# A hybrid attention/SSD trunk on one core: first modulation by feature tile, three first units side by side, and a last residual with its gates on ScalarE

## What is computed

```
mod = silu(cond) @ w_mod[l] + b_mod[l]      # 9 pieces of 1024; cond differs for context and latent
h   = rmsnorm(x, norm_pre) * (1 + scale) + shift
x   = x + 0.5 * gate * rmsnorm(swiglu(h), norm_post)
```

## Time and profile before

| | |
|---|---|
| time, median of 3 runs | 2957.63 us (2953.05 to 2960.02) |
| the profiled execution's own time | 2956.48 us |
| its span in the profile | 2954.7 us |
| mean granted TensorE clock | 0.99 of 2.4 GHz |
| TensorE matmul busy | 97% of the span |
| TensorE's share of the chain that ended last | 85% |
| VectorE / ScalarE / GpSimd busy | 59% / 37% / 9% |

### The profile page before, as it was taken

One profiled execution on the slowest core, in us unless ns is written; L12 is line 12 of the kernel. 1 busy time (PEld: TensorE's weight loads), 2 busy tenths in 40 slices (PEclk: granted clock), 3 DMA queues, 4 the chain that ended last, 5 costly groups with the idle time before them and its releaser, 6 DMA issues.

```text
span 2954.7 us, 47164 instructions
## 1 busy us (share of the span) xinstructions
PE 2854.5 (97%) x19366; PEld 2703.4 (91%) x19366; DVE 1753.5 (59%) x2640; ACT 1107.5 (37%) x1750; POOL 254.4 (9%) x201
## 2 busy tenths in 40 slices
PE   8999999998799999999999999999979999999997
PEld 5999999986589999999999999999945699999997
DVE  6567666647666555657564646457778747432334
ACT  5311126446865211146211126753334446211123
POOL 0000002000020000011000002000048511000002
PEclk9999999999999999999999999999999999999998
DMA  6545444420034544443543434632221133322233
GB/s 227 164 147 188 143 147 140 153 71 31 23 122 136 162 138 138 148 149 116 160 157 121 152 110 135 176 98 76 68 75 33 58 106 118 113 85 67 75 104 114
DMA packets 106968, 350.33 MB, mean 119 GB/s; under 512 B 11137, under 2 KB 29825, under 8 KB 106497
## 3 DMA queue, kind: packets, MB, share of 16 engines
q1 hardware_dynamic: 101122, 338.27, 36.1%
q10 hardware_dynamic: 5632, 9.05, 0.9%
HBM read 336.66 MB, written 10.62 MB: 118 GB/s over the span
## 4 chain that ended last, share of the span: by engine, by line
PE 85%; DVE 6%; ACT 3%; issue 3%; POOL 3%; DMA 0%; ACTq 0%; SPq 0%; DVEq 0%; POOLq 0%
PE P L1680 79%; PE P L1631 2%; ACT pb L884 1%; POOL mraw L687 1%; PE P L1739 1%; POOL toff L691 1%; DVE wl L1123 1%; DVE st L1253 0%; DVE xl L1163 0%; DVE xs L1425 0%; PE P L1883 0%; DVE st L1257 0%; DVE toff L1460 0%; PE P L2005 0%; DVE ft L1155 0%
## 5 line engine op out<-in xcount | busy, mean ns | idle before, releaser
L1680 PE MATMUL P<-xh,wh 128*128 128x320 f32 x4016 | 1018.4, 313 | 7.8 <-DVE xl L1163 6.6
L1680 PE MATMUL P<-xh,wl 128*128 128x320 f32 x4016 | 1005.1, 309 | 0.0
L1680 PE MATMUL P<-xl,wh 128*128 128x320 f32 x4016 | 1004.6, 309 | 0.0
L770 ACT CAST wh<-raw 128x1024 fp32r<-128x1024 f32 (+1 forms) x431 | 482.2, 1119 | 965.3 <-PE P L1680 809.0
L1123 DVE TENSOR_TENSOR wl<-raw,wh 128x1024 fp32r<-128x1024 f32 (+1 forms) x431 | 564.7, 1310 | 293.0 <-ACT wh L770 292.8
L1680 PEld LDWEIGHTS P<-xh,wh 128*128 128x128 f32 x4016 | 696.0, 188 | 16.6 <-issue 7.0
L1680 PEld LDWEIGHTS P<-xl,wh 128*128 128x128 f32 x4016 | 695.4, 188 | 2.8 <-issue 0.4
L1680 PEld LDWEIGHTS P<-xh,wl 128*128 128x128 f32 x4016 | 695.0, 188 | 0.0
L1680 PE MATMUL P<-hh,wh 128*128 128x320 f32 x1408 | 382.3, 312 | 0.0
L1680 PE MATMUL P<-hl,wh 128*128 128x320 f32 x1408 | 377.1, 308 | 0.0
L1680 PE MATMUL P<-hh,wl 128*128 128x320 f32 x1408 | 377.0, 308 | 0.0
(11 more groups left out here) (240 smaller groups left out, 2423.2 us busy)
## 6 DMA issues: line engine op xcount, KB each, us to landing
raw<-wgu_d SPq DMA_DIRECT2D x216, 512.0 KB, 3.8
mraw<-wmod_d SPq DMA_DIRECT2D x128, 512.0 KB, 3.6
raw<-wdB_d SPq DMA_DIRECT2D x64, 704.0 KB, 4.1
raw<-wdA_d SPq DMA_DIRECT2D x32, 704.0 KB, 5.4
raw<-ain_d SPq DMA_DIRECT2D x28, 512.0 KB, 3.5
raw<-sz_d SPq DMA_DIRECT2D x26, 512.0 KB, 3.9
raw<-sx_d SPq DMA_DIRECT2D x24, 512.0 KB, 3.5
raw<-aout_d SPq DMA_DIRECT2D x16, 512.0 KB, 3.5
```

The costliest lines, as they stand in the source:

```text
L770: nc.scalar.copy(wh[:, u.u % SPLITS, 0:n], raw[:, u.u % 2, 0:n]).then_inc(hi_done, 1)
L1680: ins = nc.tensor.matmul(P[:, u.banks[i], 0:C], w[:, u.u % SPLITS, k * 128:(k + 1) * 128], m[:, k, C * h:C * h + C], start=(k == 0 and w i ...
```

## The change

At the start, shifts and scales both come from TensorE, by feature tile. `cond_cols` becomes the stationary, 32 columns wide for each of the 8 input tiles (two columns used, the rest zero). For a feature tile `k`, `first_sums(k)` makes eight matmuls of 256 columns (128 shifts, 128 scales) that write to four different sets of 32 PSUM partitions in turn; ScalarE copies the 128 by 256 result (`first_copy`), and `first_turn(k)` adds the four sets and turns them to columns by two small matmuls against `pick`. VectorE makes the factors of that tile (`first_factors`). The weights (`wfirst`) come in eight loads of 1 MB, one for each feature tile. `x` is loaded by tiles, not by token halves, squared by ScalarE and VectorE in turn, and added in pairs before TensorE sums it.

The first `guA` phase has role "M" instead of "F", so its units take all 640 tokens. `first_units` has three units (`FIRST = 3`), and `first_products` of the third lags one feature tile behind the other two.

At the end of the last sub-layer ScalarE multiplies half 1 by its gates (`end_factor`), so that VectorE's `update` needs one multiplication of two tiles instead of two; a one-element Ln stands ahead of the last square, and the store of half 1 goes out in four parts, each after its pair.

```diff
-        return [Phase("guA", s, 2 * HALF[0], KD, "F", "wgu", 2 * FFT * f),
+        return [Phase("guA", s, 2 * HALF[0], KD, "F" if s else "M", "wgu", 2 * FFT * f),
...
+            sp.dma_start(cond_cols[:, :], d["cond_cols"]).then_inc(cols_in, 16)
             sp.dma_start(cond_rows[0:1, :], d["cond_rows"]).then_inc(rows_in, 16)
...
+            load_x(0)
+            load_x(1)
+            load_unit(units[0])
+            load_unit(units[1])
+            load_first(0)
             for dst, src in ((bmod[:, :, :], d["bmod"]), (npre[:, :, :, :], d["npre"]),
...
+            load_first(1)
+            load_first(2)
+            load_unit(units[2])
+            for k in range(3, KD):
+                load_first(k)
...
-            sp.wait_ge(x_ready[1], KD * (last_sub + 1))
-            sp.dma_start(d["y"][:, :, C:T], x[:, :, C:T]).then_inc(out_sem, 16)
+            for k in range(0, KD, 2):
+                sp.wait_ge(x_ready[1], KD * last_sub + k + 2)
+                sp.dma_start(d["y"][:, k:k + 2, C:T], x[:, k:k + 2, C:T]).then_inc(out_sem, 16)
...
+            def end_factor(k):
+
+                act.wait_ge(fac_ready, 2 * last_sub + 2)
+                act.wait_ge(sq_done[1], squares_before(POST, last_sub) + k + 1)
+                f = half(ft[:, k, :], 1)
+                nc.scalar.activation(f, f, ACT.Identity, scale=gp[:, k, 1:2]).then_inc(end_fac, 1)
...
             high(units[0])
...
             high(units[1])
+            first_root()
+            first_copy(0)
+            first_copy(1)
+            high(units[2])
             for k in range(KD):
-                shifted(0, 0, k)
...
+                first_shifted(k)
+                if k + 2 < KD:
+                    first_copy(k + 2)
             for u in units:
...
-                if 2 < u.u + 2 < len(units):
-                    high(units[u.u + 2])
+                if u.u != 1 and u.u + 2 < len(units):
+                    high(units[u.u + 2 if u.u else FIRST])
...
+            act.wait_ge(lg_done[1], norm_no(POST, last_sub))
+            act.wait_ge(log_in, 1)
+            nc.scalar.activation(tick[:, 0:1], eps[:, 0:1], ACT.Ln)
             post_square(last_sub, 1, units[-1], KD - 1)
+            end_factor(KD - 1)
             root(POST, last_sub, 1)
...
+            first_factors(0)
             for k in range(KD):
...
+                first_normed(k)
+                if k + 1 < KD:
+                    first_factors(k + 1)
+                if k == 0:
                     low(units[2])
-            lows(0, 0, KD - 1)
+                first_lows(k)
...
                 for k in range(KD):
-                    pe.wait_ge(xn_ready[0], k + 1)
-                    for u in us:
-                        ins = products(u, k, xh, xl)
...
+                    if k + 2 < KD:
+                        first_sums(k + 2)
+                    if k + 1 < KD:
+                        first_turn(k + 1)
+                    for h in range(2):
+                        pe.wait_ge(xn_ready[h], k + 1)
+                    for u in us[:-1]:
+                        first_products(u, k)
+                    if k:
+                        first_products(us[-1], k - 1)
+                first_products(us[-1], KD - 1)
...
+            def first_sums(k):
+
+                pe.wait_ge(first_in[k], 16)
+                if k >= 2:
+                    pe.wait_ge(first_cp, k - 1)
+                    pe.wait_ge(first_mod, k - 1)
+                for j in range(KD):
+                    r = 32 * (j % 4)
+                    ins = mm(P[r:r + 32, 6 + k % 2, 0:256], cond_cols[:, 32 * j:32 * j + 32], first_weights(k)[:, j, :],
+                             start=(j < 4), stop=(j >= 4))
+                ins.then_inc(first_sum, 1)
+
+            def first_turn(k):
+
+                pe.wait_ge(first_cp, k + 1)
+                for m in range(2):
+                    ins = mm(P[:, 6 + k % 2, 256 + 2 * m:258 + 2 * m], first_rows[:, k % 2, 128 * m:128 * m + 128], pick, start=True, stop=True)
+                ins.then_inc(first_tr, 1)
```

More of the change, by code:

```diff
@@ L194, in build @@
     for u in units:
-        if not u.place[0] and u.p.name in ("guA", "guB", "dnA"):
+        if not u.place[0] and u.p.name in ("guA", "guB", "dnA") and u.u > FIRST:
             mod_at[u.u] = list(range(t, min(2 * MT, t + (2 if u.p.name == "dnA" and u.p.s == 0 else 1))))
@@ L327, in build @@
         cols_silu = sem("cols_silu")
[L328 to L332, removed]
+        first_in = [sem("first_in%d" % k) for k in range(KD)]
+        first_sum = sem("first_sum")
+        first_cp = sem("first_cp")
+        first_tr = sem("first_tr")
+        first_mod = sem("first_mod")
+        x_even = sem("x_even")
+        x_odd = sem("x_odd")
+        x_pair = sem("x_pair")
         hi_done = sem("hi_done")
@@ L435, in made, with first_weights @@
         def made(t):
[L437 removed]
+            return 2 * (t - FIRST_MODS)
+        def first_weights(k):
+            return (mraw[:, :, :].rearrange("p a b -> p (a b)") if k == 6 else wfirst[:, k % 7, :]).rearrange("p (j c) -> p j c", j=KD)
         def two(ap):
@@ L540, in build @@
         NORMED = {0: {4: (0,), 5: (1,), 6: (2,), 7: (3,)}, 1: {6: (0,), 7: (1,), 8: (2,), 9: (3,)}}
-        FIRST_NORMED = {2 + k: k for k in range(KD)}
+        WHOLE = ((0, 0, CTX), (1, CTX, T))
         POST_TOTAL = {0: (0, 4), 1: (0, 5)}
@@ L1057, in _ @@
                     window0(s, i, (p.name, s))
-                if where == "F0" and not s and i in FIRST_NORMED:
-                    shifted(0, 1, FIRST_NORMED[i])
+                    if s == last_sub and i:
+                        end_factor(i - 1)
                 if where == "F0" and s:
@@ new lines, in first_normed @@
+            def first_normed(k):
+                if k == KD - 1:
+                    dve.wait_ge(fac_ready, 1)
+                else:
+                    dve.wait_ge(first_mod, k + 1)
+                if k == 0:
+                    for h in range(2):
+                        dve.wait_ge(rb_ready[h], 1)
+                for c, t0, t1 in WHOLE:
+                    V.scalar_tensor_tensor(ft[:, k, t0:t1], x[:, k, t0:t1], ga[:, k, c:c + 1],
+                                           rb[:, :, :].rearrange("p h c -> p (h c)")[:, t0:t1], ALU.mult, ALU.mult).then_inc(t_done[c], 1)
@@ L1497, in with_bias, with first_lows @@
+            def first_lows(k):
+                for h in range(2):
+                    dve.wait_ge(xh_done[h], k + 1)
+                for c, t0, t1 in WHOLE:
+                    V.scalar_tensor_tensor(xl[:, k, t0:t1], ft[:, k, t0:t1], mod[:, k, c:c + 1],
+                                           xh[:, k, t0:t1].bitcast(F32), ALU.add, ALU.subtract).then_inc(xn_ready[c], 1)
             def with_bias(lo, n):
@@ L1541, in _ @@
                     window1(s, i)
-                if where == "F0" and not s and i in FIRST_NORMED:
-                    normed(0, 1, FIRST_NORMED[i])
-                    if FIRST_NORMED[i]:
-                        lows(0, 1, FIRST_NORMED[i] - 1)
                 if where == "F1" and i == 0:
-                    if s:
-                        lows(s, 1, KD - 2)
+                    lows(s, 1, KD - 2)
                     lows(s, 1, KD - 1)
```

204 lines of the change are left out of this document (101 added, 103 removed).

## The result

| | before | after |
|---|---|---|
| median of this comparison | 2955.03 us (2953.05 to 2960.02, 6 runs) | 2967.91 us (2961.53 to 2969.62, 6 runs) |
| the profiled execution's own time | 2956.48 us | 2961.53 us |
| its span | 2954.7 us | 2959.7 us |
| ratio of the times | | 1.0035, 95% interval [1.0025, 1.0045] |

By it the changed kernel is slower by 0.35%, 10.3 us. It is the slower case that came, rival 2's.

What follows compares the result with a forecast made beforehand. TensorE held 85% of the chain of waits; start +4.0, clock +3 and tail -4.3 gave +2.7 us on 2956.48, and with 1.15 to the median 2960.3, rounded to 2960. The 8-in-10 range was 2949 to 2968.

Steps and rivals of the forecast that it cites:

- the slower case: Whole kernel: above 2963.5 us, through a clock staying low or column sets not overlapping; chance 0.22.
- rival 2: First stage: clock stays low, +3.5 us per step while it lasts; most of it near 2966 us; chance 0.19.
- First products: Kernel start: TensorE's first products at 28.8 us, after unit 2's landing, cast and low part; bounds 27.5 and 30.
- the ring: First stage: TensorE's products, sums and turn, then VectorE's factors and low parts, run in series without overlap, 6.0 us.
- The step: First stage, per tile: products 2.64, sums 1.15, turn 0.8, factors 0.42, low parts 1.0; 6.0 us.
- Rival 1: First stage: turn and factors overlap earlier products, steps take 4.2 us; about 2949 us, chance 0.17.
- Unit 3: End of first stage: unit 3 starts at 72.3 us after a new 1.4 us pause for cast, table load, SiLU, multiplication.
- The clock: First stage: two of six TensorE pauses bring a clock fall of up to 1.5 us each; +3, bounds 0 and +9.
- The reference start: Kernel before: product stream counted back from 53.37 by 42 products, as if begun at 47.2 us.
- The sum: Whole kernel: start +4.0, clock +3 and tail -4.3 make +2.7 us.
- Tail: Behind the last product: 0.4 from table load, 1.2 from gates, 2.7 from stores; -4.3 us, bounds -2.5 and -5.
- The sets: First-stage sums: four column sets at 79% would take 1.1 us instead of 0.87; no overlap 2972 us, chance 0.03.

Runs made afterwards that it cites:

- after_again: The changed kernel itself, unedited, timed once more; 2964.87 us, ratio 1.0031 to the kernel before.
- ring_open: The changed kernel with VectorE making the low parts of tile k before the factors of tile k+1; 2950.80 us, ratio 0.9974 to the kernel before.
- pre_silu: The changed kernel with a one-element SiLU behind the first stage's last shift, for an early table load; 2963.18 us, ratio 1.0016 to the kernel before.
- start_only: The changed kernel with the last sub-layer's end put back as it was; 2968.31 us, ratio 1.0039 to the kernel before.
- serial: The changed kernel with all eight sums of a feature tile on one set of 32 columns; 2980.66 us, ratio 1.0075 to the kernel before.
- fill: The changed kernel with three unused matmuls of 240 columns behind each turn, where TensorE waits; 2957.40 us, ratio 0.9998 to the kernel before.
- end_only: The kernel before with only the new end of the last sub-layer; 2951.66 us, ratio 0.9981 to the kernel before.
- end_stores: The kernel before with only its last store cut into four, by pairs of tiles; 2954.93 us, ratio 0.9993 to the kernel before.
- combo: The changed kernel with low parts before next factors, third unit's cast and low part later, and an early one-element SiLU; 2944.07 us, ratio 0.9958 to the kernel before.
- combo_again: The same kernel as `combo`, timed once more; 2946.20 us, ratio 0.9963 to the kernel before.

## Why the prediction was half right

**First products.** Forecast 28.8, measured 28.72, and the agreement is luck. Forecast was a chain from unit 2's landing at 25.5 through its cast and low part. In the changed kernel the cast began at 23.35, and VectorE then waited for the turn of tile 1:

```profile
23.35 1.04 ACT L783 CAST wh<-raw 128x1024 fp32r<-128x1024 f32 x1 [0.87 <-DMA raw<-wgu_d]
...
26.19 0.16 DVE L1549 TENSOR_TENSOR mod<-P,bmod 128x4 f32<-128x4 f32 x1 [1.74 <-PE P L2094]
```

So a landing 2.1 us earlier than forecast was made up by the ring, which holds tile 0 as well: the factors of tile 1 stand ahead of unit 2's low part and tile 0's. In `after_again` the sums of tile 2 ahead of that turn took 1.07 us instead of 1.66, and the first products came at 27.00, below the bound of 27.5. In `ring_open` the forecast's own chain held, from a cast at 23.47 to 27.01.

**The step.** Forecast 6.0 at full clock; measured 5.89, with products 2.88, sums 1.00 (1.15), turn 0.55 (0.8 with the hand-over), low parts 1.02 (1.0). That it is a ring, and that TensorE waits on `xl` each time, was right, and the ring is about half of what `ring_open` got back. Rival 1, that it opens by itself, did not come; `ring_open` shows that one line's place decides it.

**Unit 3.** Forecast 72.3 without falls; measured 80.03 less the excess of 8.5 is 71.5. The pause was 1.57 for 1.4, along the forecast chain.

**The clock: the step that failed.** "Of six pauses I take two, **+3**; bounds 0 and six (+9)." Five of six pauses were followed by slow products, and the term was 8.5 us, nearly its upper bound (7.7 without the sums ahead of the first pause). The mechanism stood in the text, as rival 2 with its condition "from four or more falls" and "most of it near 2966", and it was given 0.19; the error was to count the pauses of the earlier trace rows, one of two, as even odds for pauses that come again every 6 us. In `after_again` it was again five of six, in `pre_silu` four, in `start_only` and `serial` three; in `fill` and `ring_open`, which have no such pauses, none. Of the six pauses of one kernel three to five were thus followed by a fall; which ones differs between these kernels (in both profiles of the changed one it was the fourth that was followed by none), and why is open. The rule cited with rival 2 (the Trainium skill, TensorE: Matmul & The Clock Gate, section "HAM oscillation", a kernel whose bursts between waits all began at the lower clock) was nearer than my reading of the earlier trace rows, though not whole: at 58.41 us a burst ran at full clock behind the same pause. Nor does a stage wholly at the lower clock follow from it: in the kernel that the Trainium skill describes there each burst begins low but isn't low to its end, and its waits are 3 to 5 us, longer than the 2.0 here. In this stage the granted clock was 0.67 to 0.83.

**The reference start.** "42 of their 48 products behind them" was a miscount: the trace has 36 ahead of 53.37, and 36 + 2880 = 144 + 2772. The figure of before is 48.1 instead of 47.2, which made the start look 0.9 us dearer than it was. It went against the clock's error.

**The sum.** Start: forecast +4.0 + 3 = +7.0, measured +10.8: +5.5 for the clock, -0.9 for the miscount, -0.8 for a stage that was otherwise shorter (71.5 for 72.3). Tail: forecast -4.3, measured -4.7 (stores 3.1 for 2.7, gates and load 1.65 for 1.6). Not in the sum: 1.4 us that came back before 941 us. So the profiled pair differs by 10.8 - 1.4 - 4.7 and 0.3 lost behind 941 us, 5.0 us, where 2.7 was forecast.

**What stays open.** By their ratios the changed kernel lies 10.3 and 9.2 us above the kernel before, by the profiled executions 5.0 and (`after_again`) 7.8. The profiled one was the fastest of its six, and the stretch described last is a short one in it (376.2 us) and a long one in `after_again` (380.7), as long as in four of the seven edits of it where it can be read. Whether the new start makes the long one more frequent than before, or whether this is chance, these runs don't tell: with the old start there are three profiles, one short (before), one between (`end_only`, 377.8) and one long (`end_stores`, 379.6).

**The sets.** The 79% of full overlap for three sets (the Trainium skill, TensorE: Matmul & The Clock Gate, section "Measured speedup vs the span model") would have made 1.1 us of the sums; 3.57 to 1.00 is 89% of four. The measurement decides.

## What to carry to other kernels

When TensorE waits once per step, write down for each wait which instruction of its own stream must run before the awaited one can: here VectorE asked for the turn of the next tile before it gave out the present one, and one line moved was worth 14 us. Price a short pause that recurs with what the clock takes from the work behind it, as a separate term with its own experiment (`fill`), and count at least every second of the pauses that recur as followed by a fall (here three to five of six). Before a link is taken off a chain, read how long the next link on each engine is.

## What the runs showed of the hardware

**Dummy work in a pause can pay.** With three useless matmuls per step the granted clock stayed at 1.00 and the stage got 7.6 to 9.2 us shorter.

**Where executions of one kernel differ.** The runs of the kernel before spread over 12 us. In the profiles the largest difference behind the start sits in one place, the SSD scan, between two anchors of TensorE's chain near 1980 and 2355 us: 375.8 to 381.1 us in the twelve profiles where both can be read, and 376.2 and 380.7 in the two of the changed kernel. The window from 2190 to 2260 us of the kernel before (stretch 375.9):

```profile
2190.00:2260.00 70.00, 62.23 (x400) 35.88 (x400) 55.10 (x96) 30.62 (x55) 54.44 (x51) 1.00 0.18 56
```

And of `end_stores` (379.6), whose code is the same there:

```profile
2190.00:2260.00 70.00, 61.98 (x374) 35.50 (x372) 50.70 (x89) 27.52 (x50) 50.02 (x47) 0.93 0.17 53
```

In the same 70 us, as far behind each kernel's own first anchor, the granted clock was 1.00 in the four profiles with stretches up to 376.2 us (before, changed kernel, `serial`, `combo`), 0.98 and 0.95 in the two with 377.8 and 377.6 (`end_only`, `combo_again`), and 0.93 in all six with 379.6 or more. The other engines do less in a slow window, as the rows show, but not in the whole stretch: from `before` (375.9) to `after_again` (380.7) TensorE's busy time between the anchors grows from 348.4 to 354.2 us for the same work, while VectorE's (286.9 and 286.7), ScalarE's (143.2 and 143.1) and GpSimd's (134.0 and 134.1) stay. That fits the clock as the cause; it was not tried by an experiment. `combo` has a short stretch and `ring_open` a long one: at 1970 us both stand level (1970.04 and 1970.00, the 1.4 us of unit 3 being gone by then), at the second anchor `combo` leads by 5.3 (2345.85 and 2351.12). A comparison of the two spans alone would have credited the edits with that.
